# A transformer block pair on one core: 112 candidate sums instead of 256, two stores later in the load queue, the last gate's products earlier, two engines kept out of one norm

## The reference

```python
mod_x = (jax.nn.silu(c) @ ada_w[layer] + ada_b[layer])[:, None, :]
sh1, sc1, g1, sh2, sc2, g2 = jnp.split(mod_x, N_MOD, axis=-1)
...
x = x + g1 * (jnp.concatenate([pool_x, attn_x], axis=-1) @ w_out[layer])
h2 = modulate(rmsnorm_2(x, norm2_g[layer]), sh2, sc2)
x = x + g2 * peer(h2, peer_wq[layer], peer_keys[layer], peer_u[layer], peer_v[layer])

def peer(...):                                     # k = 16, 8 heads, 128 keys a side, 16384 experts
    q = (xb @ w_q).reshape(tb, PEER_HEADS, 2, PEER_DKEY // 2)
    s = jnp.einsum('thpd,hpnd->thpn', q, sub_keys)
    sv, si = lax.top_k(s, k)                       # the 16 best keys of each side
    cand = (sv[:, :, 0, :, None] + sv[:, :, 1, None, :]).reshape(tb, PEER_HEADS, k * k)
    top_v, top_i = lax.top_k(cand, k)              # the 16 best of the 256 sums
    experts = jnp.take_along_axis(cand_idx, top_i, axis=-1)
```

## Time and profile before

| | |
|---|---|
| median of 3 runs | 1430.89 us (1429.68 to 1432.53) |
| profiled execution | 1429.83 us, its span 1428.0 us |
| PE, PEld, DVE, ACT, POOL busy | 96%, 86%, 70%, 54%, 25% of the span |
| 557 to 569 us (peer norm) | PE 4.53 of 12 us busy, DVE 11.02, POOL 6.24 |
| 570 to 592 us (first query panels) | PE 15.48 of 22 us |
| 592 to 633 us (query panels) | PE 41.00 of 41 us, DVE 34.63, POOL 33.13 |
| 633 to 690 us (early units beside the select) | PE 53.96 of 57 us, DVE 51.62, POOL 49.15 |
| 690 to 714 us (end of the select) | PE 18.23 of 24 us |
| 724 to 890 us (early units and G) | PE 164.47 of 166 us |

### The profile page before, as it was taken

One profiled execution on the slowest core, in us unless ns is written; L12 is line 12 of the kernel. 1 busy time (PEld: TensorE's weight loads), 2 busy tenths in 40 slices (PEclk: granted clock), 3 DMA queues, 4 the chain that ended last, 5 costly groups with the idle time before them and its releaser, 6 DMA issues.

```text
span 1428.0 us, 21371 instructions
## 1 busy us (share of the span) xinstructions
PE 1369.0 (96%) x8444; PEld 1224.0 (86%) x8444; DVE 993.1 (70%) x1653; ACT 777.6 (54%) x1265; POOL 359.2 (25%) x210
## 2 busy tenths in 40 slices
PE   7999998999999997899799999999999999999997
PEld 6898888999978776899799999888888888888885
DVE  5676677888868648589865765766766666666666
ACT  5455745444655554354479998444445444445453
POOL 1530000000052104597722221122222222222222
PEclk9999999999999999999999999999999999999998
DMA  7653257889878424457555445566665666665665
GB/s 240 175 152 91 89 175 261 269 268 314 310 244 283 139 104 147 150 168 210 171 157 155 150 150 151 194 218 206 208 204 193 216 219 208 207 204 194 217 217 182
DMA packets 190323, 278.81 MB, mean 195 GB/s; under 512 B 9184, under 2 KB 120544, under 8 KB 189968
## 3 DMA queue, kind: packets, MB, share of 16 engines
q1 hardware_dynamic: 184640, 266.19, 57.5%
q10 hardware_dynamic: 5184, 10.02, 1.8%
q0 software_dynamic: 400, 1.25, 0.3%
HBM read 266.41 MB, written 11.01 MB: 194 GB/s over the span
## 4 chain that ended last, share of the span: by engine, by line
PE 79%; DVE 10%; ACT 4%; DMA 4%; issue 3%; POOL 1%; SPq 0%; DVEq 0%; ACTq 0%
PE bank L700 17%; PE bank L638 14%; PE bank L705 9%; PE bank L665 8%; PE bank L643 7%; PE bank L611 6%; PE bank L670 4%; PE bank L973 4%; PE bank L615 3%; DVE sb_lo L1388 2%; ACT sb_hi L1007 1%; PE bank L890 1%; DMA sb_raw<-w_in 1%; PE bank L909 1%; PE bank L787 1%
## 5 line engine op out<-in xcount | busy, mean ns | idle before, releaser
L1388 DVE TENSOR_TENSOR sb_lo<-sb_raw,sb_hi 128x1024 fp32r<-128x1024 f32 (+2 forms) x312 | 435.2, 1411 | 188.3 <-ACT sb_hi L1007 186.1
L1007 ACT ACTIVATE sb_hi<-sb_raw 128x1024 fp32r<-128x1024 f32 (+2 forms) x427 | 439.8, 1046 | 228.8 <-DMA sb_raw<-w_in 49.1
L1990 POOL TENSOR_TENSOR sb_lo<-sb_raw,sb_hi 128x1024 fp32r<-128x1024 f32 x116 | 284.7, 2461 | 723.7 <-ACT sb_hi L1007 723.6
L638 PE MATMUL bank<-sb_act,sb_hi 128*128 128x256 f32 x2240 | 299.6, 287 | 5.0 <-ACT sb_hi L1007 4.3
L638 PEld LDWEIGHTS bank<-sb_act,sb_hi 128*128 128x128 f32 x2240 | 281.9, 194 | 6.3 <-ACT sb_hi L1007 4.5
L700 PE MATMUL bank<-sb_hi,sb_hid_hi 128*128 128x512 f32 x600 | 234.1, 390 | 0.0
L700 PE MATMUL bank<-sb_hi,sb_hid_lo 128*128 128x512 f32 x600 | 234.1, 390 | 0.0
L705 PE MATMUL bank<-sb_lo,sb_hid_hi 128*128 128x512 f32 x600 | 161.3, 390 | 2.4 <-DVE sb_lo L1388 2.0
L643 PE MATMUL bank<-sb_act,sb_lo 128*128 128x256 f32 x1120 | 158.0, 284 | 5.1 <-POOL sb_lo L1990 4.4
L643 PEld LDWEIGHTS bank<-sb_act,sb_lo 128*128 128x128 f32 x1120 | 144.7, 192 | 6.1 <-POOL sb_lo L1990 5.3
L705 PEld LDWEIGHTS bank<-sb_lo,sb_hid_hi 128*128 128x128 f32 x600 | 112.4, 188 | 26.6 <-DVE sb_lo L1388 2.4
(11 more groups left out here) (328 smaller groups left out, 1589.0 us busy)
## 6 DMA issues: line engine op xcount, KB each, us to landing
sb_raw<-peer_uT SPq DMA_DIRECT2D x128, 512.0 KB, 3.9
sb_raw<-peer_v SPq DMA_DIRECT2D x128, 512.0 KB, 4.7
sb_raw<-w_in SPq DMA_DIRECT2D x52, 512.0 KB, 4.5
sb_ada_w<-ada_wT SPq DMA_DIRECT2D x48, 512.0 KB, 6.1
sb_raw<-w_gate SPq DMA_DIRECT2D x22, 512.0 KB, 4.4
sb_raw<-w_up SPq DMA_DIRECT2D x22, 512.0 KB, 4.6
sb_raw<-w_down SPq DMA_DIRECT2D x22, 512.0 KB, 4.4
sb_raw<-w_out SPq DMA_DIRECT2D x16, 512.0 KB, 4.4
```

The costliest lines, as they stand in the source:

```text
L638: e.matmul(bank[:, j * T:(j + 1) * T], hi[:, k, j * P:(j + 1) * P], part[:, k0 + k, :], start=i == first_i and j == 0 and k == 0 and part ...
L1007: e.activation(flat_of(i, "hi"), flat_of(i, "raw"), ACT.Copy).then_inc(hi_done[i % R], 1)
L1388: e.tensor_tensor(flat_of(i, "lo"), flat_of(i, "raw"), flat_of(i, "hi").bitcast(F32), ALU.subtract).then_inc(lo_done[i % R], 1)
L1990: e.tensor_tensor(flat_of(i, "lo"), flat_of(i, "raw"), flat_of(i, "hi").bitcast(F32), ALU.subtract).then_inc(lo_done[i % R], 1)
```

## The change

1. **112 sums.** `cand` has 112 columns a tile instead of 256: all sixteen columns of rows 0 to 3, and four columns of rows 4 to 15. POOL writes it in two instructions. The place of a sum is decoded by two shifts and four `scalar_tensor_tensor`, in place of a shift, an and, and a conversion.
2. **Two stores.** x and g2's row are stored behind the loads of peer_wq and the first early units, in the queue of SP, not ahead of the fourth block of peer_wq.
3. **g2's products.** Of ada_w's products the three at the last feed-forward unit and the three behind w_out2's first panel go; those behind shift up, and six (two each ahead of items 5, 9 and 13 of the second attention) come new. Rows of ada_w are loaded to match.
4. **The peer norm.** ACT rounds one block of peer_wq instead of three ahead of the norm, and POOL waits for the scaled tile (`scaled[1]`) before it splits peer_wq's second block.
5. **Two orders.** ACT's exponential of the best sums (L1321) stands ahead of the last early unit's result, instead of two units earlier. In the mix norm POOL splits one more block between its two inverse roots.

```diff
+WIDE_ROWS, NARROW = 4, 4
+N_WIDE = WIDE_ROWS * TOPK
+N_CAND = N_WIDE + (TOPK - WIDE_ROWS) * NARROW
...
-N_ADA, N_ADA_FFN = 6 * DC, 34
+N_ADA, N_ADA_FFN = 6 * DC, 31
...
-              + [(("w_gate", N_FFN - 1), 1), (("w_up", N_FFN - 1), 2)]
-              + [(("ctx_in2", 3), 2)] + [(("in2", j), 3) for j in (1, 2, 3)] + [(("w_out2", 0), 3)])
+              + [(("ctx_in2", 3), 2)] + [(("in2", j), 3) for j in (1, 2, 3)] + [(("bias", q), 2) for q in (1, 2, 3)])
...
-                hi_until(("w_out2", j))
+                hi_until(("w_out2", j), None, AHEAD if j == 0 else 1)
...
                 elif what == "E":
                     hi_until(("uT", n_e))
+                    if n_e == EARLY_BESIDE_SELECT - 1:
+                        act.wait_ge(*top_sub.at())
+                        e.activation(topv, topv, ACT.Exp).then_inc(*top_exp.inc())
                     early_out(n_e)
                     n_e += 1
-                else:
-                    if n_d == PE_H:
-                        act.wait_ge(*top_sub.at())
-                        e.activation(topv, topv, ACT.Exp).then_inc(*top_exp.inc())
-                    n_d += 1
...
                     max_of("na", i, buf)
+                    if i % 4 == 0:
+                        take_ada("bias", i // 4)
+                    if i == 12:
+                        mod_columns("g2")
...
-                    take_ada("w_out2", 0)
-                    mod_columns("g2")
...
-                own(e.tensor_tensor(ab[:, h, :, 1, :], ti, each(fifteen, NT), ALU.bitwise_and))
-                own(e.tensor_tensor(abf[:, h], ab[:, h].rearrange("p t w k -> p (t w) k"), each(nought, TW), ALU.add))
+                own(e.tensor_tensor(ab[:, h, :, 1, :], ti, each(two, NT), ALU.logical_shift_right))
+
+                row, place_in = (abf[:, h].rearrange("p (t w) k -> p t w k", w=2)[:, :, w, :] for w in range(2))
+                own(e.scalar_tensor_tensor(row, ab[:, h, :, 1, :], float(WIDE_ROWS - N_WIDE // NARROW), ab[:, h, :, 0, :], ALU.add, ALU.max))
+                e.scalar_tensor_tensor(in_row[:, 0], row, -float(TOPK), ti, ALU.mult, ALU.add)
+                own(e.scalar_tensor_tensor(in_row[:, 1], row, -float(NARROW), ti, ALU.mult, ALU.add))
+                own(e.scalar_tensor_tensor(place_in, in_row[:, 1], float(NARROW * WIDE_ROWS - N_WIDE), in_row[:, 0], ALU.add, ALU.max))
...
-            for t in range(NT):
-                inverse_rms("mix", t)
+            inverse_rms("mix", 0)
+            lo_until(("ctx_in2", 2), 2)
+            inverse_rms("mix", 1)
...
             for t in range(NT):
                 inverse_rms("peer", t)
+            pool.wait_ge(*scaled[1].at("peer", 1))
...
-                    e.tensor_tensor(cand[:, h].rearrange("p t (a b) -> p t a b", a=TOPK),
-                                    v12[:, h, :, 0, :].unsqueeze(3).to_broadcast([P, NT, TOPK, TOPK]),
-                                    v12[:, h, :, 1, :].unsqueeze(2).to_broadcast([P, NT, TOPK, TOPK]), ALU.add).then_inc(*cand_done.inc(h))
+                    for a0, a1, n, at in ((0, WIDE_ROWS, TOPK, 0), (WIDE_ROWS, TOPK, NARROW, N_WIDE)):
+                        rows = a1 - a0
+                        ins = e.tensor_tensor(cand[:, h, :, at:at + rows * n].rearrange("p t (a b) -> p t a b", a=rows),
+                                              v12[:, h, :, 0, a0:a1].unsqueeze(3).to_broadcast([P, NT, rows, n]),
+                                              v12[:, h, :, 1, 0:n].unsqueeze(2).to_broadcast([P, NT, rows, n]), ALU.add)
+                    ins.then_inc(*cand_done.inc(h))
...
             load_until(("w_out2", 1))
-            for j in range(2):
-                for t in range(NT):
-                    sp.wait_ge(*freed(("w_out2", j), t))
-            e.dma_start(parked_x.rearrange("(t p) d -> p t d", p=P), xr).then_inc(x_parked, 16)
-            for half_ in range(2):
-                sp.wait_ge(*freed("g2", half_))
-            e.dma_start(parked_g2, g2row).then_inc(g2_parked, 16)
             n_e = 0
             for what in SELECT_ORDER:
                 if what == "E":
                     load_until(("uT", n_e))
+                    if n_e == 0:
+                        for j in range(2):
+                            for t in range(NT):
+                                sp.wait_ge(*freed(("w_out2", j), t))
+                        e.dma_start(parked_x.rearrange("(t p) d -> p t d", p=P), xr).then_inc(x_parked, 16)
+                        for half_ in range(2):
+                            sp.wait_ge(*freed("g2", half_))
+                        e.dma_start(parked_g2, g2row).then_inc(g2_parked, 16)
                     n_e += 1
```

More of the change, by code:

```diff
@@ L155 @@
 HOT_BUFS = 3
+WIDE_ROWS, NARROW = 4, 4
+assert (WIDE_ROWS + 1) * (NARROW + 1) > TOPK
+N_WIDE = WIDE_ROWS * TOPK
+N_CAND = N_WIDE + (TOPK - WIDE_ROWS) * NARROW
 G_LATER = 5
@@ L518, in build @@
         i12f = place("i12f", 512).rearrange("p (h g k) -> p h g k", h=PE_H, g=TW)
-        cand = place("cand", 4096).rearrange("p (h t k) -> p h t k", h=PE_H, t=NT)
-        cand_work = place("cand_work", 512).rearrange("p (t k) -> p t k", t=NT)
+        cand = place("cand", PE_H * NT * N_CAND).rearrange("p (h t k) -> p h t k", h=PE_H, t=NT)
+        cand_work = place("cand_work", NT * N_CAND).rearrange("p (t k) -> p t k", t=NT)
+        in_row = place("in_row", 2 * NT * TOPK).rearrange("p (w t k) -> p w t k", w=2, t=NT)
         eq = place("eq", 2048).rearrange("p (b g k a) -> p b g k a", b=2, g=TW, a=TOPK)
@@ L995, in scalar_program, with hi_until @@
             let_go = set()
-            def hi_until(key, n=None):
-                end = min(span[key][-1 if n is None else n] + AHEAD, len(plan) - 1)
+            def hi_until(key, n=None, ahead=AHEAD):
+                end = min(span[key][-1 if n is None else n] + ahead, len(plan) - 1)
                 while done_hi[0] <= end:
@@ L1305, in early_out @@
                 e.dma_start(parked_units[u], early_buf[b]).then_inc(early_stored[b], 16)
-            n_h = n_e = n_d = 0
+            n_h = n_e = 0
             for what in SELECT_ORDER:
@@ L1848, in vector_program @@
             iota_p, whole = numbers[:, 0:P], numbers[:, P:P + 3].bitcast(U32)
-            four, fifteen, nought = (whole[:, i:i + 1] for i in range(3))
+            four, two, nought = (whole[:, i:i + 1] for i in range(3))
             dve.wait_ge(bank_free[b], n)
             e.tensor_copy(iota_p, iota)
-            for c, value in ((four, 4), (fifteen, 15), (nought, 0)):
+            for c, value in ((four, 4), (two, 2), (nought, 0)):
                 ins = e.memset(c, value)
```

2 lines of the change are left out of this document (1 added, 1 removed).

## The result

The changed kernel takes 1414.49 us (median of 4 runs, 1412.01 to 1416.92), the kernel before, run beside it, 1431.29 us (1429.68 to 1432.53): a ratio of 0.9892, 95% interval 0.9874 to 0.9909. Run once more with the experiments it took 1411.36 us (5 runs), ratio 0.9878 (0.9859 to 0.9898). The prediction was 1415.5 us with a range of 1403 to 1423. The profiled execution took 1416.74 us, its span 1414.9 us, 13.1 less than before.

What follows compares the result with a forecast made beforehand. PE, busy 96% of the span, was taken as the bound, so only its waits could give much. 1429.83 - 5.0 - 8.8 - 0.5 - 2.0 + 1.5 = 1415.0 us, median put at 1415.5, range 1403 to 1423.

Steps and rivals of the forecast that it cites:

- The norm: Peer norm: 5.0 us less, 2.9 from products moved off DVE and 2.1 from scaling without POOL; bounds 2.9 to 7.0.
- The query panels' start: First peer_wq blocks up to the third head's first block: 8.8 us less; bounds 6.5 and 9.5.
- The select: Shorter searches mostly eaten by small DVE instructions waiting for POOL: 0.5 us less; bounds 9.7 less and 6 more.
- The 2.3 us to be carried into the early units: Part of 13 us of DVE delay beside the query panels, expected to reach the early units.
- The later cycle: Cycle of the select's last heads: 0.5 + 1.2 - 1.65, about 0.1 us longer, not shorter.
- The first rival: Select: small decoding instructions don't wait for POOL, so it gives 9.2 us more, 1406 us; chance 22%.
- The feed-forward end: Three DVE products fewer, so PE's 2.00 us wait for a split goes: 2.0 us less; bounds 0 and 2.5.
- The second attention: Three new pairs of g2 products, 1.22 us each; one pair delays PE: 1.5 us more; bounds 0 and 4.5.
- the prediction's own sign: Second attention: the prediction is wrong if the attention grows by more than 3 us.
- the mix norm's new order: Mix norm: costs nothing; PE has no wait there, and the second root comes 2 us later with 2.8 to spare.
- The slower rival: Second attention: g2's six products all on PE's path at 3.42 us each, 20.5 us, giving 1434 us; chance 4%.
- The stores' price of nothing: Stores moved ahead of a load of peer_uT: cost nothing; 1 us if the cover is gone.

Runs made afterwards that it cites:

- shared norm: Changed kernel, but POOL splits peer_wq without waiting for the scaling and ACT rounds its first blocks ahead of the shifts: 1415.8 us, ratio 0.9908.
- decoding in PSUM: Changed kernel, with one input of each small decoding instruction in PSUM, so that none has both in SBUF: 1411.8 us, ratio 0.9872.
- g2 placed: Changed kernel, with g2's three pairs of products moved to places of the second attention where DVE was idle: 1411.4 us, ratio 0.9881.
- g2 back: Changed kernel, with g2's three feed-forward products and three behind w_out2's first panel put back, with ada_w's loads: 1414.9 us, ratio 0.9906.

## Why the prediction was right, point by point

The median lay 1.0 us below the one predicted (1.6 if the 1.06 us between the profiled execution and the median had been added in full: 1416.1). That is closer than the terms were: in the profiles they missed by 0.9, 1.2, 2.0, 0.3 and 2.3 us and left out 1.1 us elsewhere, to both sides, so part of the closeness is luck. The picks start 12.7 us earlier, where some 15 were expected.

**The norm** (-5.0, measured -5.9): both parts came as worked out, 3.0 us by the products (2.9 predicted) and 3.1 by the scaling (2.1). The second was a microsecond too small: I took half of the scaling's difference, but the turns of the second tile waited too (0.56 us more in shared norm's profile).

**The query panels' start** (-8.8, measured -7.6): the stores were the cause, as shown by putting them back. The size was off by 1.2 us, since the first blocks don't run at a block's pitch: the first starts at 567.48 and the third at 575.92, 8.4 us for two blocks and the scores, where the sum had 2 x 2.88 + 0.8 + 0.7 = 7.3. The first matmuls follow DVE's shifted values piece by piece, and the scores wait 0.73 us.

**The select** (-0.5, measured -2.5). The mechanism stands, by the decoding in PSUM: the small instructions wait for POOL, and 13.8 us of waits are there. Three sizes were wrong. Beside the query panels 13 us net were predicted for three heads; measured are 4.2 + 2.7 + 2.7 = 9.6 of waits, less 1.65 and plus 0.5 each, 6.2 net, so half. The 2.3 us to be carried into the early units don't show: DVE's wait of 4.71 us ahead of the first early unit is gone, and PE's first wait there is 0.57 us where it was 1.45. The later cycle, "0.5 + 1.2 - 1.65, about 0.1 us longer", became 0.6 shorter: the waits there are 0.4 instead of 1.2, since the candidate instructions take 0.35 us each and hold DVE only for a part of that, and DVE comes just as the last split ends. At the end, 3 us were left as gain out of the 6.0; but a wait of 3.4 us for DVE's last split took the place of the 4.31 us for ACT's rounding, which the prediction didn't see, so PE's last wait shrank by 0.9 only. The first two errors and the third have opposite signs, and that the select came near the predicted term is luck in part. The first rival (all waits gone, 9.2 us more) overpriced them: without them in the four instructions the select gives 2.2 us more.

**The feed-forward end** (-2.0, measured -1.7): PE's wait is gone. The stretch hides more: at 239 us, ahead of the stage that the change touches, the changed kernel's execution was 1.6 us later than the other (0.9 by 137 us, 0.6 with a low clock at 220 us). From there to the context panels it is 3.2 us shorter, of which 2.6 are two waits of PE for DVE's splits that are gone (2.00 and 0.61; the prediction had only the first). The other 0.6 stays open. With the products back the wait is 1.35 us.

**The second attention** (+1.5, measured +3.8). By the prediction's own sign ("if the attention grows by more than 3 us") this term failed in the profiled execution. 2.0 to 2.4 us of it are there in every profile with this code, and 1.2 to 1.9 more where the clock fell behind PE's waits. The step that failed is "POOL idles there" for the first pair: it met POOL's one split in this stage, and its first product took 2.56 us instead of 1.22. The prediction let the last pair alone cost something; it costs 0.4 us (PE waits 1.05 us for the pooled copy, 0.61 with g2 placed), and the first pair more. "The six rows of ada_w are loaded where the queue was light" overlooked that four of them go out at once ahead of a w_out2 block.

```profile
489.02 2.36 POOL L2001 TENSOR_TENSOR sb_lo<-sb_raw,sb_hi 128x1024 fp32r<-128x1024 f32 x1 [20.61 <-ACT sb_hi L1013]
489.90 2.56 DVE L1408 CUSTOM_DVE_ANT_0 sb_ada_junk<-sb_ada_w,sb_c_rows 128x1024 bf16<-128x1024 f32 x1
```

**Between feed-forward and attention** (0, measured +1.1): in all but one of the other profiles with this code it is 0.4 to 0.5, in one 1.0. In the changed kernel's profile 1.0 us of it has come by 434 us (23.59 us behind the first context matmul, 22.62 before), where PE waits for a split of POOL behind the mix norm:

```profile
433.94 1.19 PE L621 MATMUL bank<-sb_lo,sb_ctx_hi 128*128 128x512 f32 x4 [0.37 <-POOL sb_lo L2001]
```

The prediction let the mix norm's new order cost nothing. With it that split ends at 433.88 us where it ended at 431.45, and PE now comes earlier, by what it no longer waits at the end of the feed-forward stage. With g2 back PE comes 0.8 us later, and there is no such wait although the new order stays. So the two changes together make it (argued from these rows; the order alone wasn't undone).

The slower rival priced all six products at 3.42 us; one took 2.56 and five 1.22. The attention grew by 3.8 us, far from the 16.3 at which that rival would have decided. The stores' price of nothing held: with them back, PE's waits beside the early units are the same (0.57, 0.90, 0.91 and 3.40 us).

## What to carry to other kernels

A store that waits for a late result doesn't belong ahead of loads in the same queue; here it was the largest single term. When two parts of a change take away the same wait, undo both before calling either useless. The price of a small DVE instruction with two inputs in SBUF beside POOL was the time until POOL's current instruction ended, so read where it will meet it; and loads that a moved step needs are part of its price where they are bunched ahead of a block that the path wants.
